# A hybrid decoder step: v projected by token, k turned inside the projection, output projection by token chunks

## What is computed

```python
h = rms_norm(x, g_mix) * (1.0 + sc1) + sh1          # (1088 tokens, 1024)
q_sb, k_sb, v_sb, q_g, k_g, v_g, r_g, a_low = split_columns(h @ w_in)
o_sb = stick_breaking_attention(q_sb, k_all, v_all)  # 8 heads of 64; samples: past pages + new
o_g  = rms_norm(gla_chunked(q_g, k_g, v_g, log_a)) * silu(r_g)   # 4 heads, key 64, value 128
x = x + ga1 * (concatenate([o_sb, o_g]) @ w_out)
h2 = rms_norm(x, g_ffn) * (1.0 + sc2) + sh2
x = x + ga2 * (square(relu(h2 @ w_up)) @ w_down)
y = rms_norm(x, g_final)          # also returned: k_sb and v_sb by token, the gla states
```

## Time and profile before

| | us |
|---|---|
| median of 3 runs | 1931.26 |
| lowest and highest | 1928.47, 1931.32 |
| the profiled execution: time | 1928.99 |
| its span (first to last instruction) | 1927.4 |

### The profile page before, as it was taken

How to read it: one execution, slowest core, us unless ns; L and a number is a source line. 1 busy time by engine, 2 the same in 40 slices (tenths; PEclk the granted TensorE clock), 3 DMA queues, 4 the chain that set the end, 5 groups by cost and what they waited for, 6 DMA issues and landing times. The chain is left out here.

```text
span 1927.4 us, 27393 instructions
## 1 busy us (share of the span) xinstructions
PE 1689.8 (88%) x10652; PEld 1475.8 (77%) x10652; DVE 722.5 (37%) x1257; ACT 588.0 (31%) x1103; POOL 402.0 (21%) x298
## 2 busy tenths in 40 slices
PE   4799789999748888777659949999999999999996
PEld 1699767777534444345659849999999999999996
DVE  3300123434227777455811153332323232323234
ACT  4411022222117787524522242121212121212113
POOL 1011122222110000100121043232323232323230
PEclk8799979999869999867779969999999999999998
DMA  8121255553380000374061011111111111111102
GB/s 312 56 90 57 75 158 197 177 183 122 106 321 3 21 23 1 129 200 157 28 204 41 5 44 44 44 44 44 44 44 44 44 44 44 44 44 44 44 0 104
DMA packets 110933, 165.00 MB, mean 86 GB/s; under 512 B 7498, under 2 KB 72349, under 8 KB 110854
## 3 DMA queue, kind: packets, MB, share of 16 engines
q1 hardware_dynamic: 102144, 133.71, 21.2%
q0 software_dynamic: 5120, 16.78, 2.8%
q10 hardware_dynamic: 3590, 13.48, 1.7%
HBM read 138.18 MB, written 25.76 MB: 85 GB/s over the span
## 5 line engine op out<-in xcount | busy, mean ns | idle before, releaser
L389 PE MATMUL psum<-op_hi,out_hi 128*128 128x384 f32 (+1 forms) x960 | 319.8, 333 | 29.6 <-DVEq L2334 29.6
L390 PE MATMUL psum<-op_lo,out_hi 128*128 128x384 f32 (+1 forms) x960 | 314.9, 328 | 0.0
L391 PE MATMUL psum<-op_hi,out_lo 128*128 128x384 f32 (+1 forms) x960 | 314.9, 328 | 0.0
L391 PE MATMUL psum<-mlp_a_hi,out_lo 128*128 128x384 f32 (+1 forms) x768 | 251.1, 327 | 0.0
L390 PE MATMUL psum<-mlp_a_lo,out_hi 128*128 128x384 f32 (+1 forms) x768 | 250.7, 326 | 0.0
L389 PE MATMUL psum<-mlp_a_hi,out_hi 128*128 128x384 f32 (+1 forms) x768 | 250.6, 326 | 0.0
L389 PEld LDWEIGHTS psum<-op_hi,out_hi 128*128 128x128 f32 x960 | 181.7, 189 | 31.8 <-DVEq L2334 30.1
L2291 POOL TENSOR_TENSOR out_lo<-out_raw,out_hi 128x2048 fp32r<-128x2048 f32 x31 | 143.2, 4619 | 273.5 <-ACT out_hi L2311 273.5
L2340 DVE TENSOR_TENSOR mlp_sq<-mlp_relu 128x384 f32<-128x384 f32 (+1 forms) x96 | 88.2, 919 | 296.4 <-ACT mlp_relu L2324 296.4
L390 PEld LDWEIGHTS psum<-op_lo,out_hi 128*128 128x128 f32 x960 | 181.7, 189 | 1.6
L391 PEld LDWEIGHTS psum<-op_hi,out_lo 128*128 128x128 f32 x960 | 181.7, 189 | 0.0
(11 more groups left out here) (309 smaller groups left out, 2758.0 us busy)
## 6 DMA issues: line engine op xcount, KB each, us to landing
sa_k<-in_cache_k SPq DMA_DIRECT2D x64, 256.0 KB, 3.4
sa_v<-in_cache_v POOLq DMA_DIRECT2D x64, 256.0 KB, 3.8
out_raw<-in_w_up SPq DMA_DIRECT2D x16, 1024.0 KB, 5.2
out_raw<-in_w_down SPq DMA_DIRECT2D x16, 1024.0 KB, 5.0
ada_w<-in_w_ada SPq DMA_DIRECT2D x22, 512.0 KB
ada_w<-in_w_ada SPq DMA_DIRECT2D x4, 2048.0 KB, 15.5
projT<-in_stage ACTq DMA_DIRECT2D x12, 544.0 KB, 2.7
projT<-pg_stage ACTq DMA_DIRECT2D x12, 544.0 KB, 3.9
```

The lines of the kernel that those rows point to most:

```text
L389: pe.matmul(out, w_hi, x_hi, start=(k == 0), stop=False)
L390: pe.matmul(out, w_hi, x_lo, start=False, stop=False)
L391: return pe.matmul(out, w_lo, x_hi, start=False, stop=(k == nk - 1))
```

## The change

- `stage_project_in` has nine panels. q, k and the gate (9 tiles) keep the feature form; k tiles are also turned from their staging buffers between later groups, 12 turning groups in all. v and gated v (4 panels) are computed by token: 128 activations are the stationary operand and 256 weight columns the moving one, 9 token tiles per panel, and stored directly. Stores are issued by SyncE. The loops are unrolled.
- The sample attention stage has 8 tiles instead of 12, one per sample: chunk 0 in the score part (1 dense step per page), chunks 1 and 2 in the value part (2 per page). Two weight slots instead of three, two V page buffers. The new v of the samples is loaded, not turned. Tile stores are on SyncE.
- `stage_natural` is gone. The prompt attention loads q, k and v itself and builds its bias rows at its start.
- `stage_project_out_and_norm` loops over chunks outside, tiles inside; the 4 panels are loaded and split three times. The norm of chunks 0 and 1 stands between the groups of the following chunk, that of the last chunk at the start of `stage_mlp`, whose up groups now go chunk by chunk and wait for it before chunk 2.

```diff
 def stage_project_in(g, w, hT_hi, hT_lo):
+    PANELS = [(ROW_Q, PANEL), (ROW_Q + PANEL, PANEL), (ROW_K, PANEL), (ROW_K + PANEL, PANEL), (LAST, P),
+              (ROW_V, PANEL), (ROW_V + PANEL, PANEL), (ROW_VG, PANEL), (ROW_VG + PANEL, PANEL)]
...
+                    for k in range(KD):
+                        if j < NF:
...
+                        else:
+                            n = P if m < NT else TS
+                            toks = slice(m * P, m * P + n)
+                            last = three_products(pe, bank[0:n, 0:PANEL], hT_hi[:, k, toks], hT_lo[:, k, toks],
+                                                  w.hi[p % 2][:, k, :], w.lo[p % 2][:, k, :], k, KD)
+                    last.then_inc(s_mm, 1)
+                    u = (j - feature_end(4)) - 1
+                    if 0 <= u < NU:
+                        turn(u)
...
+                evacuated(sp, len(groups))
+                store_tokens(g.vgnat[0:TP, PANEL:], g.vgnat[TP:T, PANEL:], vst[1][:, :, PANEL:])
...
-def stage_natural(g, pairs):
...
-def stage_project_gla_and_sample_attention(g):
+def stage_project_gla_and_sample_attention(g, prompt):
...
-        vpg = sb("sa_v", [P, NPAGE, SB])
+        vpg = [sb(f"sa_v{i}", [P, NPAGE, SB]) for i in range(2)]
...
                 def v_pages(s):
-                    at_least(pool, s_pv, s)
-                    load_pages(pool, io["cache_v"], vpg, s, s_v)
...
+                    at_least(pool, s_pv, s - 1)
+                    load_pages(pool, io["cache_v"], vpg[s % 2], s, s_v[s % 2])
+                def low(i):
+                    pool.wait_ge(s_hi, i + 1)
+                    pool.tensor_tensor(wlo[i % 2][:], raw[i % 2][:], whi[i % 2][:], ALU.subtract).then_inc(s_lo, 1)
+                low(0)
+                v_pages(0)
+                v_pages(1)
+                for s in range(1, NSEQ):
+                    low(s)
+                    if s + 1 < NSEQ:
+                        v_pages(s + 1)
...
+                for s in range(NSEQ):
+                    if s > 0:
+                        turn_weights(s - 1)
+                    first = dense(s, [0])
+                    score(s, first)
+                    pieces(first, KD + 1)
+                    chunks = dense(s, [1, 2])
...
 def stage_prompt_attention(g, ops):
+                ops.load(sp, 0, 0)
+                ops.load_values(sp)
+                ops.load(sp, 1, 1)
...
+class SecondNorm:
+    def rstd(self, act, c, bank):
+    def normed(self, dve, j):
+    def high(self, act, j):
+    def low_dve(self, dve, j):
+    def low_pool(self, pool, j):
...
 def stage_project_out_and_norm(g, w, w_mlp, n2):
+        groups = [(c, k) for c in range(NC) for k in range(KD)]
+        def normed_at(j):
+            return [] if j < 10 or j >= NG or not 2 <= j % KD < 6 else [j - KD - 2 + j % KD - 2, j - KD - 2 + j % KD - 1]
...
+                for l in range(2, NL):
+                    sp.wait_ge(w.lo_done, l - 1)
+                    panel(l)
...
+                for l in range(2):
+                    lo(l)
+                for j in range(NG):
+                    for piece in normed_at(j):
+                        if piece % 2 == 0:
+                            n2.low_pool(pool, piece)
+                    if j % 2 and j // 2 + 2 < NL:
+                        lo(j // 2 + 2)
...
 def stage_mlp(g, w, h_hi, h_lo, n2):
-            return [(u * NUP // 2 + m * 3 + c, 2 * u + m, c) for m in range(2) for c in range(3)]
+            return [(u * NUP // 2 + c * 2 + m, 2 * u + m, c) for c in range(3) for m in range(2)]
...
+                            if c == 2:
+                                n2.wait_chunk(pe, 2)
```

More of the change, by code:

```diff
@@ L410, in _, with store_feature @@
             def _(sp):
[L411 to L416, removed]
+                def store_feature(f):
+                    evacuated(sp, feature_end(f))
+                    if f < 8:
+                        sp.dma_start(g.projT[f * P:(f + 1) * P, :], stg[f % 4][:]).then_inc(s_out[f % 4], 16)
+                    else:
+                        sp.dma_start(g.projT[ROW_A:IN_W, :], stg[0][P - RANK:P, :]).then_inc(s_out[0], 16)
@@ L424, in _ @@
[L424 to L430, removed]
+                for p in range(1, NP):
+                    n = PANELS[p][1]
+                    pool.wait_ge(w.hi_done, p + 1)
+                    pool.tensor_tensor(w.lo[p % 2][:, :, 0:n], w.raw[p % 2][:, :, 0:n], w.hi[p % 2][:, :, 0:n],
+                                       ALU.subtract).then_inc(w.lo_done, 1)
@@ L448, in _, with bank_free @@
[L448 to L463, removed]
-                        t0, tw = CHUNKS[c]
[L465 to L473, removed]
+                def bank_free(j):
+                    if j >= NB:
+                        pe.wait_ge(s_ev[j % 2], (j - NB) // 2 + 1)
@@ L475, in _, with in_order @@
+            def in_order(mine, group, k_turn, extra):
+                for j in range(len(groups)):
+                    extra(j)
+                    if j % 2 == mine:
+                        group(j)
+                    u = j - feature_end(4) - 1
+                    if 0 <= u < NU and u % 2 == mine:
+                        k_turn(u)
             @block.vector
             def _(dve):
-                evacuate(dve, dve.tensor_copy, 1, s_dev, True)
+                group, k_turn = evacuate(dve, dve.tensor_copy, 1)
+                in_order(1, group, k_turn, lambda j: None)
@@ L515, in _, with round_hi @@
[L515 to L521, removed]
+                def round_hi(p):
+                    n = PANELS[p][1]
+                    act.wait_ge(w.loaded[p % 2], 16 * (p // 2 + 1))
+                    if p >= 2:
+                        act.wait_ge(s_mm, panel_end(p - 2))
+                    act.copy(w.hi[p % 2][:, :, 0:n], w.raw[p % 2][:, :, 0:n]).then_inc(w.hi_done, 1)
@@ L524, with split @@
+                starts = {panel_end(p - 2) if p >= 2 else 0: p for p in range(1, NP)}
+                def split(j):
+                    if j in starts:
+                        round_hi(starts[j])
+                group, k_turn = evacuate(act, act.copy, 0)
+                in_order(0, group, k_turn, split)
 class PairOperands:
@@ L871, in _, with score @@
                 last.then_inc(s_zn, 1)
[L873 to L875 removed]
+                def score(s, between):
+                    slot = s % 2
                     at_least(pe, s_x, s)
[L877 removed]
+                    pe.wait_ge(s_k[slot], s // 2 * 128 + 128)
                     for half in range(2):
[L879 removed]
+                        pe.matmul(Z[:, half * 512:half * 512 + 512], bst[:].rearrange("o p c -> o (p c)"), ones, start=True, stop=False,
                                   skip_group_check=True)
@@ L951, in dense @@
                             yield
[L953 to L966 removed]
+                for s in range(NSEQ):
+                    if s > 0:
+                        turn_weights(s - 1)
[3 more added lines that the diff above has]
+                    chunks = dense(s, [1, 2])
+                    if s > 1:
+                        turn_out(s - 2, s % 2)
+                    if s > 0:
+                        values(s - 1, (s - 1) % 2, chunks)
+                    pieces(chunks, 2 * KD + 1)
                 turn_weights(NSEQ - 1)
@@ L1211, in _ @@
             def _(pool):
-                for p in range(2, NPAIR):
+                pool.memset(ops.bias[:].bitcast(F32), 0.0).then_inc(ops.s_bz, 1)
+                for p in range(NPAIR):
                     ops.scale(pool, p, p % 2)
@@ L2164, in _ @@
+                    for piece in normed_at(j):
+                        if piece % 2:
+                            n2.low_dve(dve, piece)
             @block.tensor
```

793 lines of the change are left out of this document (376 added, 417 removed).

## The result

The kernel after takes 1949.05 us (median of 4 runs, 1944.94 to 1953.84), the kernel before 1930.3: a ratio of 1.0099, 95% interval 1.0072 to 1.0127. The kernel is slower by about 1%, as forecast (1948). The profiled execution of the kernel after took 1944.94, span 1943.3, against 1928.99 and 1927.4: +15.9 between the spans.

What follows compares the result with a forecast made beforehand. TensorE, busy 88% of the span, was taken as the bound where dense. Terms 64.1 + 12.6 - 38.7 - 19.6 = +18.4 us led to a forecast of 1948 us, 8-in-10 range 1926 to 1965.

Steps and rivals of the forecast that it cites:

- Input projection: Feature tiles go from 13 to 9 (-47.3 us), 864 matmuls of 256 columns are added (+103.1); with turnings and stores +64.1.
- Sample attention: Sample attention stage: four gated v tiles leave (-47.3 us), but stalls and lost clock come in their place; +12.6 in all.
- The six waits: Samples 2 to 7: TensorE's first dense step waits for GpSimd's split behind eight v page loads, 9.5 us each, +57.0.
- The end term: End of sample attention: values(7) no longer waits for its pages, thanks to the second v buffer; -9.4 us.
- The start term: Start of sample attention: four turnings of the new v at half clock and the copy behind them go; -1.5 us.
- Rival A: Sample attention: GpSimd's queue does not reach TensorE, so 70.8 us of stall and clock go; 1877 us, chance 0.07.
- Turning stage: The stage of exposed loads and stores goes (45.6 us), but attention starts with its own loads (6.9); -38.7.
- Output projection: Output projection and norm: most idle behind the projection goes (-27.6 us), against +8 of waits; -19.6.
- The 8 us of waits: Output projection: VectorE instructions with two SBUF inputs meet GpSimd's split and delay TensorE's sums of squares; bounds 2 and 15.
- Rival D: Sample attention: the stalls come, but the clock recovers at once and the bubbles are 2 us; 1928 us, chance 0.08.
- rival B: Input projection: 256-wide products with activations as weights cost as much as 384-wide ones; +46.6, 1994 us, chance 0.05.
- rival C: Output projection: reloaded panels are late at every pair, by 1.5 us and some clock; +15, 1963 us, chance 0.10.

Runs made afterwards that it cites:

- two_products: The kernel after with the product of high activations by low weights left out of the token groups of v and gated v: 1909.36 us.
- low_first: The kernel after with GpSimd's low part of tile s issued ahead of the V page loads of sample s, not behind them: 1877.99 us.
- one_v: low_first with one V page buffer instead of two: 1891.05 us, ratio 0.9783 to the kernel before.
- best: low_first and psum_tmp together, with GpSimd's first split issued behind the page loads of sample 0: 1872.59 us.
- psum_tmp: The kernel after with the output projection's scaled sample part written back to PSUM, so VectorE's addition has one SBUF input: 1943.26 us.
- out_alone: The kernel before with only the kernel after's output projection, norm and MLP start: 1913.62 us, ratio 0.9914.

## Why the prediction was right, step by step

**Input projection**, +62.2 for +64.1. The term that could have been far off was the 256-wide matmul: 0.1175 us, where the line through the earlier trace rows gave 0.1193. Over 864 of them that is 1.6 of the 1.9 us of difference. two_products shows that the panels' loads and splits have no part in this term. The formula that the prediction quotes, and set aside, gave 109 ns; measured are 117.5.

**Sample attention**, +14.0 for +12.6. The six waits were worked out as 9.5 us each and are 9.7 on average (57.0, measured 58.4). The clock was put at 2.3 each (13.8) and low_first shows 2.0 (11.75); the 2.3 was a choice between bounds, and of these the lower is mis-sized, since 3 us at half speed lose 1.5 and not 1.7. The end term was -9.4; one_v shows -12, because values(7) also ran at half clock there, which the earlier trace rows had to be read for (3.64 us for 64 matmuls that take 1.95 at full clock). The start term was put at -1.5 and is +2.4: the first score comes 322.29 - 297.95 = 24.34 us behind the stage's first load, before 254.47 - 232.48 = 21.99. The turnings of the new v are gone, but the first split now stands beside VectorE's subtraction. In best, where it does not, the first score comes 320.64 - 298.46 = 22.18 us behind the first load, so that this accounts for 2.2 of the 3.9 us by which the term was off; the rest is open. What remains for the four tiles is 14.0 - 58.4 - 11.75 + 12.2 - 2.4 = -46.4, against the 47.3 of the forecast. The terms were off by 0.9 to 3.9 us each and cancel: that the sum is off by only 1.4 is in part luck. Rival A, by which the queue does not reach TensorE, was wrong for this order and is right for another. 1877 was its price, and low_first, which makes it true, took 1878.

**Turning stage**, -39.6 for -38.7, seen in the trace alone. No experiment undid this part.

**Output projection**, -19.0 for -19.6. The sum was right, and one of its terms was right in size and kind, but not in place. The 8 us of waits were placed at the end of chunk 1 (4.4) and in chunk 2 (3.5), by norm pieces on VectorE. In the trace there is no wait in chunk 1, one of 1.39 in chunk 2 and one of 4.10 behind the last group, and both come from the small addition L2171. The norm's multiplication does take 4.43 us beside a split in chunk 1, but the sum of squares of a group stands behind the next group on TensorE, and these 5 us cover it. With 2.2 us of smaller gaps the groups take 121.5 us instead of 117.9, and the end 8.3 instead of 30.6; the MLP's first matmul waits 1.95 behind the last sum of squares, forecast 2. The term of 8 us thus measures 3.6 + 4.1 = 7.7. psum_tmp shows that the mechanism was the right one (VectorE with two inputs in SBUF beside a split). The walk through the queues had the instruction and the places wrong, and that its sum fits so well is luck.

**What was in no term**: -3.0 in attention and gla, of which 2.1 lie in the prompt attention (225.7 us from first score to the first matmul of gla, 227.8 before), and -2.0 in MLP and final. The first is no effect of the change: with the same code from the first score on, the stretch takes 397.57 us in the profile of the kernel after and 399.5 to 403.8 in those of the six experiments on it, and with the old code 400.58 and 404.55 (before and out_alone). The second is small: eight profiles with the new start of the MLP lie at 787.98 to 790.06, the one with the old at 791.07. Why is open. Together with the head (+3.3), these stretches nearly cancel in the profiled pair (-1.7).

Rival D (the clock recovers at once) falls with the fences on the clock, rival B with the spacing, and rival C with the absence of any wait for a panel's low part beyond the first one.

## What to carry to other kernels

Read a queue for what stands behind its blocking instruction: a load that waits for a buffer delays everything issued after it in the same queue. Here a split of 2.4 us behind eight such loads stopped TensorE for 9.7 us per sample. The same loads one place later did not stop it at all. When a step is moved to the start of a loop, look up where in its queue the work for it stands.

An instruction with both inputs in SBUF on VectorE can last until GpSimd's instruction beside it ends (an addition of 0.22 us took 4.31). Where it stood on the path, taking one input from PSUM removed that.

## What was not expected of the hardware

- VectorE instructions without two SBUF inputs are not all exempt. In the profile of one_v a cast of 64 elements from SBUF (one input) that began 0.6 us behind the start of GpSimd's split took 2.14 us, where two such casts together take 0.44 in best. The cast ends with the split, at 309.40 and 309.35. Instructions with one input in PSUM kept their time in the output projection: 0.47 to 0.62 us in all 24 scaled additions (L2173) of the kernel after, by width, and 0.22 to 0.23 in the eight additions of psum_tmp.

```profile
307.26 2.14 DVE L1014 CAST sa_bias_rows<-sa_w 1x64 fp32r<-1x64 f32 x1
```

- The clock's price behind a wait of 5.1 us was 2.4 us, behind one of 9.7 us 1.9: the slow stretch was longer behind the shorter wait, in five cases of six.
